# Expert weights of a two-layer diffusion trunk loaded as row pairs, and a first projection done chunk by chunk

## The reference, cut to what matters

```python
h2 = rms_norm(x, lw['norm2_g']) * (1 + sc2) + sh2
aff = jax.nn.softmax((h2 @ router), axis=-1)
gate, idx = lax.top_k(jnp.swapaxes(aff, 1, 2), cap)      # cap = 64 latent, 16 context
xe = h2[idx]
a = jnp.einsum('ecd,edf->ecf', xe, w_gate)               # w_gate, w_up: 16 x 1024 x 1024
b = jnp.einsum('ecd,edf->ecf', xe, w_up)
ye = jnp.einsum('ecf,efd->ecd', jax.nn.silu(a) * b, w_down) * gate
out = jnp.zeros_like(h2).at[idx].add(ye)
```

## Time and profile before

| | |
|---|---|
| median of 3 runs | 2074.49 us (2068.59 to 2078.87) |
| the profiled execution, whole | 2072.48 us |
| its span, first to last instruction | 2070.3 us |
| busy: TensorE, VectorE, ScalarE, GpSimd | 93%, 26%, 22%, 8% |
| chain that ended last, by engine | TensorE 65%, DMA 15%, SP's queue 9%, VectorE 5% |
| HBM read | 506.59 MB |

### The profile page before, as it was taken

One profiled execution on the slowest core, in us unless ns is written; L12 is line 12 of the kernel. 1 busy time (PEld: TensorE's weight loads), 2 busy tenths in 40 slices (PEclk: granted clock), 3 DMA queues, 4 the chain that ended last, 5 costly groups with the idle time before them and its releaser, 6 DMA issues.

```text
span 2070.3 us, 36301 instructions
## 1 busy us (share of the span) xinstructions
PE 1930.2 (93%) x14878; PEld 1070.2 (52%) x14878; DVE 533.8 (26%) x1187; ACT 450.6 (22%) x947; POOL 160.7 (8%) x140
## 2 busy tenths in 40 slices
PE   4999998995999999999989999989699999999996
PEld 3756677872443434343466657778534344434342
DVE  1166124533111111111131832263511111101013
ACT  3131233231111112121132214332212121212112
POOL 0000001100101010101000000020000101111110
PEclk8999999997999999999999999999799999999998
DMA  8313122447999999999934122215659999999996
GB/s 313 102 60 105 43 80 85 155 154 270 391 389 390 392 389 394 390 393 390 397 114 140 46 82 81 82 65 193 233 215 393 390 393 385 397 385 397 385 395 239
DMA packets 172886, 532.96 MB, mean 257 GB/s; under 512 B 17296, under 2 KB 50192, under 8 KB 172560
## 3 DMA queue, kind: packets, MB, share of 16 engines
q1 hardware_dynamic: 155248, 493.53, 61.8%
q0 software_dynamic: 11712, 22.29, 4.9%
q10 hardware_dynamic: 5856, 16.16, 2.0%
HBM read 506.59 MB, written 25.33 MB: 257 GB/s over the span
## 4 chain that ended last, share of the span: by engine, by line
PE 65%; DMA 15%; SPq 9%; DVE 5%; issue 4%; ACT 1%; DVEq 0%
PE wide L1240 12%; DMA ring<-w_up 12%; PE wide L837 9%; PE wide L827 8%; SPq L644 7%; PE wide L1248 6%; PE wide L1120 6%; PE narrow L1271 6%; PE wide L1284 3%; DMA ring<-w_down 2%; PE turned L786 2%; PE narrow L758 2%; PE wide L956 1%; DMA ring<-w_mod 1%; PE narrow L1143 1%
## 5 line engine op out<-in xcount | busy, mean ns | idle before, releaser
L1240 PE MATMUL wide<-ring,ht 128*64 128x512 f32 x2048 | 454.1, 599 | 9.5 <-DMA ring<-w_up 5.0
L1240 PEld LDWEIGHTS wide<-ring,ht 128*64 128x64 f32 x2048 | 143.6, 138 | 304.6 <-issue 278.3
L1271 PE MATMUL narrow<-ring,ht 128*64 128x512 f32 x1024 | 234.3, 599 | 1.9 <-DMA ring<-w_down 1.9
L1248 PE MATMUL wide<-ring,ht 128*32 128x256 f32 x4096 | 234.3, 380 | 0.0
L2207 DVE TENSOR_TENSOR ht<-ht,wide 128x512 f32<-128x512 f32 x64 | 35.5, 555 | 679.6 <-ACT ht L1765 459.2
L837 PE MATMUL wide<-stream,ht 128*128 128x256 f32 (+1 forms) x960 | 194.0, 364 | 3.5 <-DVE ht L1866 3.5
L837 PEld LDWEIGHTS wide<-stream,ht 128*128 128x128 f32 x960 | 170.5, 191 | 25.8 <-issue 5.1
L1248 PEld LDWEIGHTS wide<-ring,ht 128*32 128x32 f32 x4096 | 126.6, 110 | 108.2 <-issue 31.3
L827 PE MATMUL wide<-ht,stream 128*128 128x128 f32 (+1 forms) x640 | 175.7, 435 | 0.0
L1765 ACT ACTIVATE ht<-wide 128x512 f32<-128x512 f32 x32 | 19.1, 597 | 623.0 <-PE wide L1240 623.0
L2413 POOL DMA_INDIRECT moe_sums<-ht x60 | 93.3, 1555 | 712.6 <-DVE ht L2224 637.4
(11 more groups left out here) (282 smaller groups left out, 1532.8 us busy)
## 6 DMA issues: line engine op xcount, KB each, us to landing
ring<-w_gate SPq DMA_DIRECT2D x256, 512.0 KB, 12.4
ring<-w_up SPq DMA_DIRECT2D x256, 512.0 KB, 14.2
ring<-w_down SPq DMA_DIRECT2D x128, 1024.0 KB, 20.0
stream<-w_mod SPq DMA_DIRECT2D x38, 1024.0 KB, 5.5
stream<-w_in SPq DMA_DIRECT2D x20, 1024.0 KB, 7.3
ring<-w_mod SPq DMA_DIRECT2D x10, 1024.0 KB, 19.0
stream<-w_out SPq DMA_DIRECT2D x6, 1024.0 KB, 6.2
moe_sums<-x ACTq DMA_DIRECT2D x10, 512.0 KB, 4.3
```

The lines of the kernel that those rows point to most:

```text
L1240: ins = mm(psW[h * 64:(h + 1) * 64, 0, w * HALFW:(w + 1) * HALFW], xT[:, k, 0:CAPS], ring[:, k, w, h * HALFW:(h + 1) * HALFW], start=(k == ...
L1248: ins = mm(psW[q * STRIP:(q + 1) * STRIP, 1, w * QW:(w + 1) * QW], xT[:, k, CAPS:SLOTS], ring[:, k, w, q * QW:(q + 1) * QW], start=(k == 0 ...
L1271: ins = mm(psN[c * 64:(c + 1) * 64, 0, :], hmT[:, j, h_ * 64:(h_ + 1) * 64], ring[:, KD + k // 2, k % 2, c * HALFW:(c + 1) * HALFW], start ...
```

## The change

All three expert matrices are loaded as pairs of neighbouring rows: partition p of a slot gets rows 2p and 2p+1 of a block of 256 rows, 8 KB in one piece. A pair of slots (2j, 2j+1) now holds 256 rows of `w_gate` and of `w_up`; slots 8 to 11 hold 256 rows of `w_down` each. TensorE waits for, and SP reloads, gate and up slots two at a time. Since chunk (c, r) now means the rows 256c + 2n + r, everything that meets these weights is written in that order: the token rows, the silu and the product read with a step of two elements, and the shift and scale columns of groups 3 and 4 are made a second time in paired order (three more matmuls and one more copy for each group). The router's parameter block shrinks from 32 to 16 columns. Apart from that, the first projection goes chunk by chunk over the four latent tiles, with the last transposes between the chunks.

```diff
-            def load_gateup(l, e, k):
-                for i, w in enumerate(("w_gate", "w_up")):
-                    src = io[w][bass.ds(l, 1), bass.ds(e, 1), k * P:(k + 1) * P, :]
-                    sp.dma_start(ring[:, k, i, :], src.rearrange("l e p n -> (l e p) n")).then_inc(s_slot[k], 16)
...
             def load_slot(l, e, slot):
...
+                weights, pair = (io[("w_gate", "w_up")[slot % 2]], slot // 2) if slot < KD else (io["w_down"], slot - KD)
+                src = weights[bass.ds(l, 1), bass.ds(e, 1), 2 * P * pair:2 * P * (pair + 1), :]
+                sp.dma_start(ring[:, slot].rearrange("p r n -> p (r n)"), src.rearrange("l e (p r) n -> (l e p) (r n)", r=2)).then_inc(s_slot[slot], 16)
...
-                    for k in range(KD):
-                        sp.wait_ge(s_gu_used, (l * EXPERTS + e) * KD + k + 1)
+                    for pair in range(KD // 2):
+                        sp.wait_ge(s_gu_used, (l * EXPERTS + e) * KD + 2 * pair + 2)
                         settle(sp)
-                        load_gateup(l, e, k)
+                        load_slot(l, e, 2 * pair)
+                        load_slot(l, e, 2 * pair + 1)
...
             def load_head(l, u):
-                sp.wait_ge(s_gu_used, l * EXPERTS * KD + slot + 1)
+                sp.wait_ge(s_gu_used, l * EXPERTS * KD + 2 * (slot // 2) + 2)
...
             def mod_columns(l, g):
...
+                if g in ROUTING_GROUPS:
+                    o = bank(N, job)[:, 2 * KD:4 * KD]
+                    i = ROUTING_GROUPS.index(g)
+                    mm(o, ident, par("bmodp")[:, KD * i:KD * (i + 1)].unsqueeze(2).broadcast_to([P, KD, 2]), start=False, stop=False)
+                    for b in range(NG):
+                        ins = mm(o.rearrange("p (q b c) -> p b q c", q=PARTS, b=NG)[:, b], mod_rows[:, g % 2, :].rearrange("p (n r) -> p r n", r=2)[:, b],
+                                 con("strips").rearrange("p (q c) -> p q c", q=PARTS), start=False, stop=(b == NG - 1))
...
+            def norm_into_mla(l, which):
+                w = next_unit(l)
+                W.claim(pe, l, "mla_a.s")
+                o = bank(W, "mla_a.s")
+                for k in range(KD):
+                    if k == 2:
+                        W.taken(pe, l, f"{which}.w1")
+                    if k >= 4:
+                        T.taken(pe, l, f"{which}.{k}")
+                    for t in range(TS):
+                        ins = mm(o[:, t * GW:(t + 1) * GW], hT[:, k, t * P:(t + 1) * P], w[:, k, 0:GW],
+                                 start=(k == 0 and t % 2 == 0), stop=(k == KD - 1 and t % 2 == 1))
+                    if k in (1, 2):
+                        turn_sample(l, which, 5 + k)
+                    if k in (4, 5):
+                        turn_prompt(l, which, k - 4)
+                W.finish(ins)
...
             def latent_gate_up(m):
                 for k in range(KD):
-                    pe.wait_ge(s_slot[k], (m + 1) * 32)
+                    if k % 2 == 0:
+                        for w in range(2):
+                            pe.wait_ge(s_slot[k + w], (m + 1) * 16)
...
             def mod_out(l, g):
+                if g in ROUTING_GROUPS:
+                    N.wait(act, l, f"modc.{g}")
+                    A((shift2p, sc2p)[ROUTING_GROUPS.index(g)].rearrange("p k c -> p (k c)"), bank(N, f"modc.{g}")[:, 2 * KD:4 * KD], ACT.Identity)
...
-                            A(xn[:, t, :], x[:, t, :], ACT.Identity, scale=rstd[:, t:t + 1]).then_inc(s_rows_ready, 1)
+                            A(in_chunks(xn[:, t, :]), paired(x[:, t, :]), ACT.Identity, scale=rstd[:, t:t + 1]).then_inc(s_rows_ready, 1)
...
-                        A(hm, psW[:, 0, 0:HALFW], ACT.Silu).then_inc(s_silu, 1)
+                        A(in_chunks(hm), paired(psW[:, 0, 0:HALFW]), ACT.Silu).then_inc(s_silu, 1)
...
-                V.tensor_tensor(h, h, up, ALU.mult).then_inc(s_hm, 1)
+                V.tensor_tensor(in_chunks(h), in_chunks(h), paired(up), ALU.mult).then_inc(s_hm, 1)
...
                         scales(l, A2, modT[:, 4 * KD:5 * KD, :], par("n2g"))
+                        scales(l, A2p, sc2p, par("n2p"))
```

More of the change, by code:

```diff
@@ L376, in build @@
         A2 = carve(sb("scale2", KD * 2), 0, KD, 2)
+        pairs_r = sb("pair_cols", 3 * KD * 2)
+        shift2p, sc2p, A2p = (carve(pairs_r, i * KD * 2, KD, 2) for i in range(3))
         small_r = sb("stats", NSMALL)
@@ L774, in mod_columns @@
                     ins = mm(o.rearrange("p (q b c) -> p b q c", q=PARTS, b=NG)[:, b], mod_rows[:, g % 2, b * P:(b + 1) * P],
-                             con("strips").rearrange("p (q c) -> p q c", q=PARTS), start=False, stop=(b == NG - 1))
+                             con("strips").rearrange("p (q c) -> p q c", q=PARTS), start=False, stop=(b == NG - 1 and g not in ROUTING_GROUPS))
+                if g in ROUTING_GROUPS:
[5 more added lines that the diff above has]
+                                 con("strips").rearrange("p (q c) -> p q c", q=PARTS), start=False, stop=(b == NG - 1))
                 N.finish(ins)
@@ L806, in turn_sample, with turn_prompt @@
                 transposes(l, job, [(o[:, t * P:(t + 1) * P], xn[:, t, k * P:(k + 1) * P]) for t in range(TS)])
[L808 to L816, removed]
+            def turn_prompt(l, which, i):
+                job = f"{which}.{KD + i}"
+                if i == 0:
+                    pe.wait_ge(s_xn, (l + 1) * (NT - ACT_TILES))
+                o = bank(T, job)
+                transposes(l, job, [(o[:, j * P:(j + 1) * P], xn[:, CTX, (4 * i + j) * P:(4 * i + j + 1) * P]) for j in range(4)])
+            def norm_into_mla(l, which):
[15 more added lines that the diff above has]
+                W.finish(ins)
+                for k in (KD, KD + 1):
+                    T.taken(pe, l, f"{which}.{k}")
+                W.claim(pe, l, "mla_a.p")
+                for k in range(KD):
+                    ins = mm(bank(W, "mla_a.p")[:, 0:GW], hT[:, k, SAMPLE:NTOK], w[:, k, 0:GW], start=(k == 0), stop=(k == KD - 1))
+                W.finish(ins)
             def feature_major(l, g):
@@ L1176, in router_bias @@
             def router_bias(l):
-                rt = par("router", KD, STRIP)
+                rt = par("router", KD, EXPERTS)
                 N.taken(pe, l, "modc.3")
@@ L1248, in context_gate_up @@
                             ins = mm(psW[q * STRIP:(q + 1) * STRIP, 1, w * QW:(w + 1) * QW], xT[:, k, CAPS:SLOTS],
-                                     ring[:, k, w, q * QW:(q + 1) * QW], start=(k == 0 and w == 0), stop=(k == KD - 1 and w == 1))
+                                     gate_up(k, w)[:, q * QW:(q + 1) * QW], start=(k == 0 and w == 0), stop=(k == KD - 1 and w == 1))
                     ins.then_inc(s_gu_used, 1)
@@ L1757, in gathered @@
                             ins = A(xT[:, k, lo:lo + n], bank(T, job)[:, k * GROWS + lo:k * GROWS + lo + n], ACT.Identity,
[L1758 removed]
+                                    scale=A2p[:, k, s_:s_ + 1], bias=shift2p[:, k, s_:s_ + 1])
                     T.take(ins, job)
@@ L2134, in route_weights @@
             def route_weights(l):
-                rt = par("router", KD, STRIP)[:, :, 0:EXPERTS]
-                dve.wait_ge(s_scale, 2 * l + 2)
+                rt = par("router", KD, EXPERTS)[:, :, 0:EXPERTS]
+                dve.wait_ge(s_scale, 3 * l + 2)
                 for s_ in range(2):
@@ L2215, in gathered @@
                         ins = V.tensor_scalar(xT[:, 4 + k, lo:lo + n], bank(T, job)[:, k * GROWS + lo:k * GROWS + lo + n],
-                                              A2[:, 4 + k, s_:s_ + 1], modT[:, 3 * KD + 4 + k, s_:s_ + 1], ALU.mult, ALU.add)
+                                              A2p[:, 4 + k, s_:s_ + 1], shift2p[:, 4 + k, s_:s_ + 1], ALU.mult, ALU.add)
                 T.take(ins, job)
@@ L2490, in everywhere, with paired_columns @@
         return np.repeat(v.reshape(DEPTH, 1, -1), P, axis=1)
+    def paired_columns(v):
+        return v.reshape(DEPTH, -1, P, 2).transpose(0, 2, 1, 3)
+    put("n2p", paired_columns(a["norm2_g"]))
+    put("bmodp", paired_columns(a["b_mod"][:, 3 * D:5 * D]))
     for name, key in (("n1g", "norm1_g"), ("n2g", "norm2_g"), ("bmod", "b_mod"), ("sgg", "sg_norm_g"), ("convb", "conv_b"),
```

37 lines of the change are left out of this document (15 added, 22 removed).

## The result

The changed kernel took 2063.04 us (median of 9 runs, 2058.14 to 2068.04) beside 2073.0 for the kernel before (9 runs, 2064.8 to 2079.8): a ratio of 0.9944, 95% interval [0.993, 0.9958], or 11.6 us less (8.7 to 14.5); the two medians differ by 10.0. A second series of the same kernel gave 0.9952 [0.9936, 0.9969], 10.0 less. The prediction was 2067 within 2057 to 2080. The profiled execution took 2058.14, with a span of 2056.3.

What follows compares the result with a forecast made beforehand. Expert stage bound by TensorE (33.49 us per expert) early in a layer, then by weight loads (34.0). Terms: 2072.5 - 11.0 (experts) - 5.0 (projection) + 3.4 (columns) + 7.0 (packets) = 2066.9, say 2067 us; range 2057 to 2080.

Steps and rivals of the forecast that it cites:

- faster: Whole kernel: a time below 2062.1 us, beyond the 0.5% (10.4 us) a measurement can tell; chance 0.33.
- The forecast's own case: Whole kernel: the summed terms hold, giving 2066.9, say 2067 us; chance 0.50.
- The experts: Expert stage, both layers: 8 KB loads cut 34.0 us per expert to 33.3, ending TensorE's waits; -11.0 us.
- Rival (b): Weight loads: pair packets bring no rate, TensorE still waits 11.0, pair waits cost up to 4.4; 2075.3 us, chance 0.13.
- The larger packets: Ahead of expert 0: the token-row store, beside 8 KB weight packets, lands later; +7.0 us for both layers.
- packets alternate one to one whatever their size: Two busy DMA queues: a 4 KB queue beside 8 KB weights falls from half the bytes to a third.
- Rival (a): Ahead of expert 0: the token-row store is not slowed, the sum without 7.0; 2059.9 us, chance 0.27.
- The columns: Groups 3 and 4: three more matmuls and one more copy cost 1.75 us per layer; +3.4 us.
- The step of two: Token rows, silu and product: strided reads taken as 0, with +4 us kept for the range.
- The first projection: Start of each layer: chunk-by-chunk projection begins earlier, with transposes between chunks, saving 2.5 us per layer; -5.0 us.
- Layer 1 has the same sequence: First projection: the 2.5 us saving found in layer 0 was taken for layer 1 too.
- Rival (c): Expert loop: the gather of every expert comes late, 2.5 us for 14 experts in each layer; 2137 us, chance 0.10.

Runs made afterwards that it cites:

- columns_five: Changed kernel with the three matmuls of the second set of columns issued five times, groups 3 and 4, both layers: 2081.41 us, 1.0029 of the kernel before.
- pairs_only: Changed kernel with the old first projection (all transposes first), keeping pair loads and second set of columns: 2075.98 us, 1.0009 of the kernel before.

## Why the prediction was right, point by point

The time lay in the range, 4 us under the forecast; the change was just over the 0.5% that the text called faster, and in the second series just under. The forecast's own case came true: all four mechanisms are there. The sizes hit less well: the sum had 5.6 us of gain, and 10.0 to 11.6 were measured, about twice as much. That the time still fell into a range of 23 us is in part luck. Term by term:

- *The experts*, -11.0: measured 11.2, with every period at 33.48 and no weight load in the chain. Packets of 8 KB took 305 ns for the estimated 302. By that count alone (1.4% less per byte) 34.0 would have become 33.6 and not the 33.3 of the text, still over TensorE's 33.49; over the longer stretch the queue's time per byte fell by 3.8%, which is enough. Rival (b) fell. The 4.4 us that rival (b) put on the pair waits where loads are slow was 4.1 with 4 KB packets, more loads included. The Trainium skill, HBM Reference, Specifications (TRN2), which the prediction cited for 358 GB/s, says behind its table that a core streaming alone gets about 425, bounded by its DMA engines; that sentence, not the figure alone, agrees with the 430 GB/s here.
- *The larger packets*, +7.0: measured 8.7. The step "packets alternate one to one whatever their size" is seen as such (220 beside 215). By layer the term was off, +4.7 and +3.5 for 6.3 and 2.3: in layer 0 the gather was late as well, which the prediction had only as its upper bound, and in layer 1 the store was 1.5 later, not 3.5. Rival (a) fell. The Trainium skill, DMA: Bandwidth & Descriptors, Queues, rings and completion order, has each engine turn between queues packet by packet; the equal counts above agree.
- *The columns*, +3.4: 4.0 per set by `columns_five` (2.8 to 5.3), where part is the clock; 2 to 4 without the set.
- *The step of two*, 0: the product unchanged, the row tiles 0.44 longer, at most 0.8 us of the gaps in all. The 1.7 times that the prediction took from the Trainium skill, Vector Engine (DVE) Microarchitecture Reference, on the SBUF access granule, would have been 9.0 (its rows of 1.73 and 1.054 ns per column make 1.64 times, 8.7). The page is on VectorE, and ScalarE's rows here took 1.08 times.
- *The first projection*, -5.0: **this is the step that failed in size.** Alone it is worth 8.7 (6.0 to 11.6). In layer 0 the first feature-major block came 2.5 earlier, as predicted: at 72.8 on the mean of eleven profiles, for 75.3 on the mean of three. "Layer 1 has the same sequence" was wrong: there the stretch behind the modulation's block (L758, L760 after) shortened by 5.6, of which 3.0 are the order of the work, as predicted, and 2.6 the clock, since between the layers TensorE had also been running at 1.2 GHz behind its idle stretches. The trace of before shows it (0.72 granted in 1060 to 1072), and the sum had no term for it. The 2.5 and the 5.6 make 8.1 of the 8.7. Another 1.6 of the difference between the first two profiles, in the block ahead, is an accident of the execution.

The terms as measured make -11.2 - 8.7 + 8.7 + 4.0 = -7.2; the whole was -10.0 and -11.6 in its two series. With the loads in place the projection is worth more than alone (from 1.0009 to 0.9944 or 0.9952, 12 to 13 us). In `pairs_only` the old projection took 29.47 us for the 27.89 of the kernel before, at a lower clock, which may be part of it. This remainder of 3 to 4 us isn't settled; the stretches where the clock comes and goes differ by as much from one execution to the next. Rival (c) fell too: the gathers of all experts landed in a median of 7.4 for 7.1, and the experts kept TensorE's pace.

## What to carry to other kernels

A larger packet is faster for its own queue and takes a larger part of every engine from all queues beside it; look for the one small, urgent transfer that shares a stretch with the loads, and hold the loads that aren't urgent, which in the best of three ways tried was worth as much as the whole change (10 to 11 us by the ratios, and 2 to 5 in the two others). When a load-bound stage turns compute-bound, expect the gain once (11 us) and look at once for where it is paid back. An overlap that closes an idle stretch of TensorE can be worth about twice its own time, if the granted clock was low behind that stretch (3.0 and 2.6 us here). And before a shorter stretch is put down to an edit, see whether the part that shortened lies behind the edit.

## What the runs showed of the hardware that was not expected

- Two queues share an engine by packets, not by bytes, also at 8 KB against 4 KB: 220 packets beside 215, 1.67 MB to 0.88 MB in 6 us.
- TensorE's clock fell from 2.4 to 1.2 GHz while it was busy without a gap, in a row of matmuls of 8 and 16 columns, and stayed there for some 7 us (0.66 granted in 284 to 288, 0.50 in 288 to 292).
- The same kernel took 373.3 and 377.5 us for the same stretch in two executions, at a granted clock of 0.99 and 0.97.
- A step of two on ScalarE's input cost 8% (5.75 for 5.31 us); on VectorE's PSUM operand nothing (0.69 and 0.69).
